# One gather for two items, up blocks with u and g in turn, and a rearranged end, in a decoder trunk on one core

## The reference

```python
def swiglu(x, w13, w2):
    g, u = jnp.split(x @ w13, 2, axis=-1)
    return (jax.nn.silu(g) * u) @ w2

def moe_swiglu(xn, router_w, w13, w2):            # 8 experts, width 3584
    logits = (xt @ router_w).astype(jnp.float32)
    top_vals, top_idx = lax.top_k(logits, TOP_K)
    top_p = jax.nn.softmax(top_vals, axis=-1)
    gates = jnp.sum(jax.nn.one_hot(top_idx, N_EXPERTS) * top_p[..., None], axis=1)
    for e in range(N_EXPERTS):
        out = out + gates[:, e:e + 1] * swiglu(xt, w13[e], w2[e])

for layer in range(2):
    x = x + hybrid_mixer(rmsnorm(x, ...), ...)
    x = x + memory_cross_attention(rmsnorm(x, ...), mem_n, ...)
    x = x + (swiglu if layer == 0 else moe_swiglu)(rmsnorm(x, ...), ...)
return rmsnorm(x, final_norm_g)
```

## Time and profile before

| | us |
|---|---|
| median of 3 runs | 1345.71 (1344.3 to 1346.89) |
| the profiled execution's own time | 1345.04 |
| its span, first to last instruction | 1343.2 |
| PE busy in the span | 1321.8 (98%) |
| instructions in the trace | 29602 |
| ACT, DVE busy | 331.0, 408.6 |
| all 16 DMA engines, queue q1 | 81.4% of the span |

### The profile page before, as it was taken

The page is one execution under the profiler, slowest core; times in us unless marked ns, Lnnn a source line. Parts: engine busy times, 40 slices in busy tenths (PEclk is TensorE's granted clock), DMA queues, the critical chain, the costliest instruction groups (busy, mean ns, idle before and its releaser), DMA issues.

```text
span 1343.2 us, 29602 instructions
## 1 busy us (share of the span) xinstructions
PE 1321.8 (98%) x13165; PEld 1047.9 (78%) x13165; DVE 408.6 (30%) x773; ACT 331.0 (25%) x616; POOL 14.8 (1%) x28
## 2 busy tenths in 40 slices
PE   9999999999999999998999999999999999999996
PEld 6989888888798989654988898666898666898652
DVE  6686764444758754000101100101100100100101
ACT  6565554443646542000001000000000000000001
POOL 1100000000000000000000000000000000000000
PEclk9999999999999999999999999999999999999999
DMA  8935355555544679999999999999999999999995
GB/s 315 341 135 215 99 195 189 188 189 188 181 155 152 240 305 396 380 420 420 420 420 419 420 410 364 411 421 420 419 421 418 421 420 421 419 418 420 420 421 213
DMA packets 63931, 444.57 MB, mean 331 GB/s; under 512 B 7293, under 2 KB 8717, under 8 KB 10936
## 3 DMA queue, kind: packets, MB, share of 16 engines
q1 hardware_dynamic: 61976, 437.22, 81.4%
q0 software_dynamic: 1824, 5.42, 1.2%
HBM read 441.17 MB, written 1.44 MB: 330 GB/s over the span
## 4 chain that ended last, share of the span: by engine, by line
PE 90%; DMA 4%; SPq 3%; DVE 2%; issue 1%; ACT 1%; DVEq 0%; ACTq 0%
PE bank L2079 49%; PE bank L1637 10%; PE bank L1639 10%; PE bank L1638 10%; SPq L495 3%; PE bank L2031 2%; DMA slot_w_hi<-in_moe_units 2%; DMA slot_xT_lo<-in_moe_units 2%; PE bank L2145 2%; PE bank L1732 1%; PE bank L1679 1%; DVE w_lo L977 1%; PE bank L2056 1%; PE bank L2057 1%; PE bank L1867 1%
## 5 line engine op out<-in xcount | busy, mean ns | idle before, releaser
L977 DVE TENSOR_TENSOR w_lo<-raw,w_hi 128x1024 fp32r<-128x1024 f32 x154 | 181.6, 1219 | 42.3 <-ACT w_hi L617 41.5
L1547 DVE TENSOR_TENSOR hidden<-hidden,bank 128x384 f32<-128x384 f32 (+1 forms) x56 | 27.3, 488 | 545.7 <-ACT hidden L921 545.7
L617 ACT ACTIVATE w_hi<-raw 128x1024 fp32r<-128x1024 f32 x154 | 155.1, 1058 | 47.7 <-PE bank L1639 47.6
L921 ACT ACTIVATE hidden<-bank 128x384 f32<-128x384 f32 (+1 forms) x56 | 24.5, 438 | 395.0 <-PE bank L2079 395.0
L2079 PE MATMUL bank<-raw,mid_x 128*32 128x128 f32 (+1 forms) x1680 | 97.4, 380 | 0.0
L2079 PEld LDWEIGHTS bank<-raw,mid_x 128*32 128x32 f32 x1680 | 93.4, 110 | 3.3 <-issue 2.8
L912 ACT ACTIVATE hT<-bank 128x384 f32<-128x384 f32 (+1 forms) x56 | 24.5, 438 | 287.0 <-PE bank L2145 287.0
L1637 PE MATMUL bank<-xT_hi,w_hi 128*128 128x256 f32 x320 | 91.6, 286 | 0.0
L1638 PE MATMUL bank<-xT_lo,w_hi 128*128 128x256 f32 x320 | 90.5, 283 | 0.0
L1639 PE MATMUL bank<-xT_hi,w_lo 128*128 128x256 f32 x320 | 90.5, 283 | 0.0
L2079 PE MATMUL bank<-raw,hT 128*32 128x256 f32 (+2 forms) x760 | 88.2, 486 | 1.8 <-DMA raw<-in_moe_units 1.7
(11 more groups left out here) (340 smaller groups left out, 2037.5 us busy)
## 6 DMA issues: line engine op xcount, KB each, us to landing
raw<-in_moe_units SPq DMA_DIRECT2D x109, 1024.0 KB, 23.8
slot_w_hi<-in_moe_units SPq DMA_DIRECT2D x47, 1024.0 KB, 23.1
slot_w_lo<-in_moe_units SPq DMA_DIRECT2D x46, 1024.0 KB, 23.1
raw<-in_layer_units SPq DMA_DIRECT2D x44, 1024.0 KB, 5.3
raw<-in_dense_units SPq DMA_DIRECT2D x33, 1024.0 KB, 5.2
slot_bias<-in_moe_units SPq DMA_DIRECT2D x19, 1024.0 KB, 23.0
slot_xT_lo<-in_moe_units SPq DMA_DIRECT2D x19, 1024.0 KB, 23.8
slot_qk<-in_moe_units SPq DMA_DIRECT2D x18, 1024.0 KB, 22.7
```

The source lines that it names most:

```text
L617: act.activation(w_hi[:, st.split(u), half, :], raw[:, st.slot(u), half * n:(half + 1) * n], ACT.Copy)\
L921: act.activation(hidden[:, 0:n * P], bank[2][:, 0:n * P], ACT.Silu).then_inc(sem("silu"), 1)
L977: dve.tensor_tensor(w_lo[:, st.split(u), half, :], raw[:, st.slot(u), half * n:(half + 1) * n], w_hi[:, st.split(u), half, :].bitcast(F32) ...
L1547: dve.tensor_tensor(hidden[:, 0:n * P], hidden[:, 0:n * P], bank[j % 2][:, 0:n * P], ALU.mult)\
```

## The change

1. **Units.** `expert_units` cuts the expert's up blocks in another way: a unit holds 2 of the 8 contraction blocks and 1024 columns, in which 128 of u and 128 of g take turns. A step still has 4 up units and 2 down units of 1 MB.
2. **Banks.** Banks 0 and 1 become one tensor, `up_banks`. u and g of a step go there side by side (mid: 768 columns, few: the 512 of bank 0), each step into the same place. Bank 2 becomes free.
3. **Order of a step.** `between` and the transposes of step j-1 stand ahead of all of step j's up units, since these write over what `gated` reads.
4. **Gather.** For items 2 and 3, 4 and 5, 6 and 7 one `gather_pair` picks 96 and 64 rows at once into banks 2, 6 and 7, at the end of the item before the pair. ACT copies in six pieces (`pair_in`). Item 1's gather moves to step 1 of item 0.
5. **The norms.** `root` has one chained operation fewer; `half_means` writes one more small column.
6. **The end.** `last_return` with the four products (and a fifth) stands in a branch for "no overflow" ahead of the loop; ACT's squares and guesses likewise. The fourth quarter is weighed by the gain ahead of time (`weigh_x`, `weighed_y`) in a fifth accumulation in bank 0, so that ACT can finish it by one scaled copy beside DVE's third quarter.

```diff
+def expert_units(w13, w2):
+    def ups(j):
+        cols = [c + j * FT + b * P + np.arange(P) for b in range(FT // P) for c in (FE, 0)]
+        both = w13[:, np.concatenate(cols)]
+        return [unit(both, 2 * m, 2, 0, 2 * FT) for m in range(KD // 2)]
...
+    up_banks = ctx.enter_context(nc.psum_tensor("up_banks", [P, 1024], F32))
+    bank = [up_banks[:, 0:512], up_banks[:, 512:1024]]
+    weighed_bank = 0
+    pair_banks = (2, 6, 7)
...
+        def pair_in(n):                                        # ACT
+            for g, b in enumerate(pair_banks):
...
+                act.wait_ge(sem("gather_mm"), 3 * n + 4 + g)
+                act.activation(mid_x[:, k, :], both[:, :, 0:MID], ACT.Copy)
+                last = act.activation(few_x[:, k, :], both[:, :, MID:MID + FEW], ACT.Copy)
...
-            c.link(dve.scalar_tensor_tensor(newton[:, a], mean[:, a], r0[:, a], r0[:, a], ALU.mult, ALU.mult))
-            c.link(dve.tensor_scalar(newton[:, a], newton[:, a], -0.5, 1.5, ALU.mult, ALU.add))
-            last = dve.tensor_tensor(rstd[:, a], r0[:, a], newton[:, a], ALU.mult)
+            c.link(dve.scalar_tensor_tensor(newton[:, a], neg_mean[:, a], r0[:, a], r0[:, a], ALU.mult, ALU.mult))
+            last = dve.scalar_tensor_tensor(rstd[:, a], newton[:, a], 1.5, r0[:, a], ALU.add, ALU.mult)
...
+        def gather_pair(n):                                    # PE
+            pe.wait_ge(sem("select"), n + 3)
+            pe.wait_ge(sem("spread"), 2 * n + 2)
+            for k in range(KD):
+                out = bank[pair_banks[k // 3]][:, (k % 3) * (MID + FEW):(k % 3 + 1) * (MID + FEW)]
+                for t in range(NT):
+                    mm = pe.matmul(out, xn[:, t, k * P:(k + 1) * P], S2[:, t, :], start=(t == 0), stop=(t == NT - 1))
...
+        def few_up(w, k, start, stop):
+            a = (k % 2) * 1024
+            for half in range(2):
+                mm = product(bank[0][half * FEW:(half + 1) * FEW, :], few_x[:, k, :], w[:, a + half * 512:a + (half + 1) * 512],
+                             start, stop)
...
+        def mid_up(w, k, start, stop):
+            a = (k % 2) * 1024
+            rows = [mid_x[:, k, g * 32:(g + 1) * 32] for g in range(3)]
             for g in range(3):
+                product(bank[0][g * 32:(g + 1) * 32, :], rows[g], w[:, a:a + 512], start, stop)
+            for g in range(2):
+                product(bank[0][96:128, g * 256:(g + 1) * 256], rows[g], w[:, a + 768:a + 1024], start and g == 0, stop)
             for g in range(3):
+                product(bank[1][g * 32:(g + 1) * 32, 0:256], rows[g], w[:, a + 512:a + 768], start, stop)
+            return product(bank[1][96:128, 0:256], rows[2], w[:, a + 768:a + 1024], start, stop)
...
             for j in range(begin + 1, end):
-                e = 6 * j - 2
-                up(e, j % 2, j - 1)
-                up(e + 2, 2)
+                if between is not None:
+                    between(j)
+                turn_hidden(j - 1)
+                up(j)
                 pe.wait_ge(sem("turned"), steps_done(i, j - 1))
                 down(j - 1, 0)
...
+        def last_return():
+            pe.wait_ge(sem("last_y"), 1)
+            for n, b in enumerate(last_banks):
...
+            pe.wait_ge(sem("weighed_y"), 1)
+            pe.matmul(bank[weighed_bank][:, :], spread[r, 1, P:2 * P].bitcast(F32), weighed_y[r, :], start=False, stop=True,
+                      skip_group_check=True).then_inc(sem("last_out_mm"), 1)
+        with pe.If(n_items < NE + 1):
+            last_return()
         with pe.If(n_items > NE):
...
+            act.activation(xn[:, 1, 512:1024], bank[weighed_bank][:, :], ACT.Copy, scale=rstd[:, 1:2])\
+                .then_inc(sem("last_piece"), 1)
```

226 lines of the change are left out of this document (129 added, 97 removed).

## The result

| | before | after |
|---|---|---|
| median, us | 1344.77 (6 runs, 1344.27 to 1346.89) | 1337.91 (6 runs, 1337.25 to 1339.15) |
| profiled execution | 1345.04 | 1339.15 |
| its span | 1343.2 | 1337.3 |
| instructions in the trace | 29602 | 24948 |

A forecast was written before the change was run, and what follows sets the result against it. It took PE's work between 632.57 and 841.86 us (ring full) and the unhidden tail as bounds. Terms -2.75 + 0.6 + 0 - 0.3 - 0.2 - 1.35 = -4.0 from 1345.04 gave 1341.0, median 1341.7; range 1338.5 to 1345.0.

The forecast's parts named there:

- The gathers: Between 632.57 and 841.86 us on PE, two gathers become one pair's gather of 4.5 us: -2.75 us (-3.6 to -1.9).
- rival A: Transfer dip at 780 to 860 us has another limit, so the gather's gain misses the stream: 1343.9 us, chance 0.16.
- The wait moved: Transposes ahead of a step's up units: wait for silu and gate exposed only in first steps; +0.6 us (0 to 1.5).
- Rival C: One pair of up banks makes PE wait ahead of up units in all 12 mid steps; 1348.9 us, chance 0.08.
- The units themselves: New mid up units take PE as long as the old, few units wait for the stream: 0, +-0.5 us.
- Rival D: Gather costs 3.6 us and the fetch more, or wide up products run nearer the streaming limit: 1339.4 us, chance 0.15.
- Instructions: 15% fewer instructions to fetch, 1.0 us, about a third where the stream is saturated: -0.3 us (0 to -1.0).
- (a): Tail: PE's return follows last_y in line, without the 0.97 us at the branch over the overflow loop: -0.85 us (0 to -0.9).
- (b): Tail: two Newton steps in the chain each 0.19 us shorter, second half_neg adds 0.07: -0.3 us.
- (c): Tail: ACT scales the fourth quarter beside DVE's third, so SP issues its transfer sooner: -0.2 us.
- rival B's second form: Tail: code fetch returns behind last_norm through ACT's far branch, cancelling the branch gain: 1342.6 us, chance 0.15 for both forms.
- (d): Tail: weighing y, the fifth product and moved lay_x hide beside other work or PE's wait: 0, up to +0.5 us.

The follow-up runs named there:

- two kernels with an early jump: Changed kernel with PE's code from item 7's step 5 (or step 2) and return at program end, jumping there over the overflow loop: 1338.24 and 1336.77 us.

## Why the prediction was right in direction and wrong in size

**The gathers: right.** Forecast -2.75 (4.5 for the pair). One gather of 4.44 us stands for 3.64 + 3.61: -2.81; at 160 columns the streaming sets it (0.139 us each, 0.87 ns a column) and not the 0.113 us spacing. The kernel before with the new order has a stretch of 209.69 us and the changed kernel with the fourth group in 128s one of 206.93; what mainly tells them apart are the gathers: -2.76. That the gain reaches the stream, which rival A denied, the doubled first gather showed.

**The wait moved: right.** Forecast +0.6 (0 to 1.5). The order alone cost 0.40 in the stretch, 0.2 of it in item 0's body. In item 0's head the gather covers it; without that it showed 1.24 us. Rival C, a wait in every step, is absent.

**The units themselves: the step that failed.** I wrote "no difference, 0", having compared a down unit (2.60) with an up unit (2.61) by their mean pace, and named +-0.5. The cost of the old pattern does not show in that pace but once a step, at the hand-over from column groups to the full array: the fourth group ends 0.19 us behind the others, and the transposes wait for it. With the new pieces of 256 columns it is 0.07, and 0.19 - 0.07 = 0.12 is the step's gain of 0.11: 13 x 0.11 = -1.43 us, shown from the other side by the kernel that brings the 128s back. Rival D had that size (1.4 us for wide up products) by a price per unit that isn't there, which is luck. My +-0.5 came from the difference of two means, and was no bound on an effect at the end of a pattern.

**Instructions: the mechanism right, the term mis-sized.** I took 15% of the queue's time and called a third of it exposed: -0.3. The queue went from 105 packets to 87 (-17%), but the 10 fetches that went from the saturated stream are worth 0.084 us each, -0.84 over 250 to 430 MB. Both factors were low: not a third of the missing fetches lay there but 10 of 18, and each cost more than its 1.07 / 16 us. The Trainium skill (Runtime: NRT & Kernel Launch, "Instruction fetch mechanics") calls the cost of crossing a 16 KiB boundary "mostly hidden". For PE that agrees, since the few unit in quarters, with four times the products, took 1.75 us in place of 1.72; the stream of weights on the same DMA engines paid it. Between item 3's first unit and the last the profile of after gained 1.6 us; of the other 0.8, 0.3 lie ahead of 250 MB and 0.5 behind 430. The kernel with few products in quarters loses the 0.5 again, so it too seems to go with the instructions, but no experiment tells how.

**The norms: not seen ahead of the experts.** Forecast -0.2; with the old norms the median was the same within 0.6 us. The 0.5 us gained ahead of the stretch is less than the start varies.

**The tail: each step right, the end given back.** (a) -0.93 for -0.85. Steps (b) and (c) with it brought the last output's issue from 11.15 to 9.61 us behind the last unit, -1.54 against -1.35. Step (b) alone is shown by the old norms, 0.3. Then the output lands 0.6 to 1.3 us later where a fetch meets the outputs. That is rival B's second form ("the fetch of the code comes back"), except that it is PE's branch and not ACT's: with the overflow code left out on PE alone the loss is gone. I had priced (a) as if a branch that nobody waits for were free. (d) was right, PE still waits 0.41 us for the last unit; but the picture behind it, PE ahead of the stream from 842 us on, was not: PE works off a backlog there until 1284, and its waits behind that, 4.9 us, are what it can take. 8.9 us are too many.

So of the profiled execution's 1339.15 against the forecast's 1341.0, -1.85 us: -1.43 is the units, -0.2 the wait, -0.06 the gathers, -0.5 the fetches, +1.3 the tail, +0.1 what is around the span; -0.3 ahead of the stretch and -0.8 behind it stay open. The error on the medians is 3.8 because I added 0.67 for the median of the three runs I was shown, and the profiled execution of after lay 1.24 above its own median. The 0.67 was chance: the median of six runs of before is 1344.77, 0.27 below the profiled execution.

## What to carry to other kernels

Compare two product patterns not by their mean pace but where the pattern ends: read the time from the last unit's start to the next full-array instruction, and look whether one column group starts its last piece later than the others. In a saturated stream, count the instruction fetches and multiply by what two traces with different counts show for one. A branch moved off the critical chain still fetches code: ask which transfers it meets, and put it where its engine still has time to make up the pause; how much it has, its waits for the stream up to the end tell.

## What the runs showed of the hardware

- A column group whose pieces were 128 columns wide, 0.109 us apart, ended 0.19 us behind groups with pieces of 384 in the same unit (0.07 with pieces of 256), and the transposes of the full array waited for it (2.87 against 2.75 us).
- A 16 KB instruction fetch took 1.07 us on one DMA engine and cost a stream of 420 GB/s 0.084 us.
- PE's taken branch over the loop took 3.64 us before and 3.85 after (3.35 to 4.35 in the eleven profiles that have it at the end), with the DMA engines mostly idle, and 6.07 and 6.01 us in the full stream (from 1288.4 and from 1250.3 in the two kernels with an early jump). PE stood still for less, 4.35 and 1.76 us, since products issued before it ran on.
- PE's granted clock fell behind the pause of 4.35 us (0.54 over the next 5 us) and stayed at 1.00 behind that of 1.76 us (the window from 1258 us).
